# Values as the stationary operand, in two halves of the array's columns, in attentions A and C

## The reference

```python
def gqa_attend(q, k, v, mask=None, sink=None):
    s = jnp.einsum("btkgd,bskd->bkgts", q, k).astype(jnp.float32) * (q.shape[-1] ** -0.5)
    ...
    if sink is not None:
...
    else:
        p = jax.nn.softmax(s, axis=-1)
    o = jnp.einsum("bkgts,bskd->btkgd", p.astype(v.dtype), v)
```

## Time and profile before

| | us |
|---|---|
| median of 3 runs (5578.72 to 5581.25) | 5580.46 |
| the profiled execution | 5575.79 |
| its span | 5574.2 |
| PE busy | 4813.2 (86%) |
| PEld busy | 4151.0 (74%) |
| DVE busy | 3091.8 (55%) |
| ACT busy | 2596.6 (47%) |
| values' sum of A and C, line 837: 3904 PE records | 468.3 busy |
| transposes' copy on ACT, line 882: 288 | 216.5 busy |
| mean granted clock of PE | 0.935 |

### The profile page before, as it was taken

How to read it: one execution, slowest core, us unless ns; L and a number is a source line. 1 busy time by engine, 2 the same in 40 slices (tenths; PEclk the granted TensorE clock), 3 DMA queues, 4 the chain that set the end, 5 groups by cost and what they waited for, 6 DMA issues and landing times. The chain is left out here.

```text
span 5574.2 us, 82058 instructions
## 1 busy us (share of the span) xinstructions
PE 4813.2 (86%) x28941; PEld 4151.0 (74%) x28941; DVE 3091.8 (55%) x4784; ACT 2596.6 (47%) x3436; POOL 1159.4 (21%) x1097
## 2 busy tenths in 40 slices
PE   5788889889799986899992888999989998599994
PEld 0688878779687875787772888998878777487773
DVE  1655145666544443777766551557663433677775
ACT  0444245556423321777762442555652322477773
POOL 0444200340000001333333441004200000333332
PEclk7899999999899997999996999999989998799997
DMA  8533462313433364899986533424153325799997
GB/s 371 193 94 97 165 213 59 80 47 100 155 124 145 143 217 144 332 397 397 397 330 239 171 95 92 109 57 109 50 159 132 134 90 205 259 397 397 397 397 285
DMA packets 597494, 1111.13 MB, mean 199 GB/s; under 512 B 112560, under 2 KB 295632, under 8 KB 589104
## 3 DMA queue, kind: packets, MB, share of 16 engines
q1 hardware_dynamic: 551760, 956.16, 49.4%
q0 software_dynamic: 29504, 94.50, 4.3%
q10 hardware_dynamic: 16032, 57.88, 2.6%
HBM read 907.97 MB, written 200.45 MB: 199 GB/s over the span
## 5 line engine op out<-in xcount | busy, mean ns | idle before, releaser
L658 PE MATMUL project_proj_acc<-project_w_split,project_hT 128*128 128x256 f32 x5472 | 726.8, 293 | 0.0
L658 PEld LDWEIGHTS project_proj_acc<-project_w_split,project_hT 128*128 128x128 f32 x5472 | 696.2, 199 | 0.3 <-issue 0.2
L1538 PE MATMUL merge_acc<-merge_hT,merge_w_split 128*128 128x512 f32 (+1 forms) x2880 | 641.3, 377 | 36.4 <-DMA merge_hT<-hT 30.4
L1538 PEld LDWEIGHTS merge_acc<-merge_hT,merge_w_split 128*128 128x128 f32 x2880 | 506.6, 191 | 146.7 <-issue 29.7
L2185 DVE TENSOR_TENSOR experts_w_gate<-experts_raw_gate,experts_w_gate 128x2048 fp32r<-128x2048 f32 x148 | 373.5, 2531 | 356.1 <-ACT experts_w_gate L2137 355.9
L937 DVE TENSOR_REDUCE attend_stat<-attend_scores 128x1 f32<-128x1280 f32 (+2 forms) x288 | 305.9, 1062 | 325.2 <-PE attend_scores L852 324.2
L2122 POOL TENSOR_TENSOR experts_w_down<-experts_raw_down,experts_w_down 128x2048 fp32r<-128x2048 f32 x74 | 361.4, 4884 | 534.3 <-ACT experts_w_down L2137 534.3
L837 PE MATMUL attend_out_acc<-attend_values,attend_probsT 128*128 128x64 f32 x3904 | 468.3, 271 | 0.1
L837 PEld LDWEIGHTS attend_out_acc<-attend_values,attend_probsT 128*128 128x128 f32 x3904 | 459.3, 192 | 0.4 <-ACT attend_probsT L882 0.4
L2232 PE MATMUL experts_gate_acc<-experts_w_gate,experts_rowsT 128*128 128x512 f32 x1776 | 438.2, 402 | 12.3 <-DVE experts_rowsT L2190 6.0
L2246 PE MATMUL experts_result_acc<-experts_w_down,experts_hiddenT 128*128 128x512 f32 x1776 | 436.8, 401 | 12.2 <-DVE experts_w_down L2185 12.2
(11 more groups left out here) (207 smaller groups left out, 8079.1 us busy)
## 6 DMA issues: line engine op xcount, KB each, us to landing
experts_raw_gate<-in_w_exp_gate_dram SPq DMA_DIRECT2D x148, 1024.0 KB, 13.9
experts_raw_up<-in_w_exp_up_dram SPq DMA_DIRECT2D x148, 1024.0 KB, 12.9
experts_raw_down<-in_w_exp_down_dram SPq DMA_DIRECT2D x148, 1024.0 KB, 11.3
merge_w_raw<-in_w_merge_dram SPq DMA_DIRECT2D x120, 768.0 KB, 6.2
modulation_w_ada<-in_w_ada_dram SPq DMA_DIRECT2D x48, 1024.0 KB, 27.1
qk<-project_staged SPq DMA_DIRECT2D x168, 256.0 KB, 2.3
attend_keys<-qk SPq DMA_DIRECT2D x128, 320.0 KB, 5.7
ye<-experts_result ACTq DMA_DIRECT2D x74, 512.0 KB, 6.2
```

What stands on the lines that cost most here:

```text
L658: m = pe.matmul(acc[s % 4][:, 0:HALF], hT[:, a, k, t * P:(t + 1) * P], w_split[hf][:, c, k, :], start=(i == 0 and k == 0), stop=(i == 2 an ...
L1538: m = pe.matmul(acc[:, b, 0:w], w_split[b][:, a, k, :], hT[:, x, k, 0:w], start=(i == 0 and k == 0), stop=(i == 2 and k == KD - 1))
```

## The change

The values' product changes sides. Before, the transposed probabilities (128 keys x 128 queries) were loaded as the stationary operand and the values (64 columns) streamed through; the sum came out as 128 queries x 64. Now the values (64 columns) are stationary, in the left half of the array's columns for even key tiles and in the right half for odd ones, and the probabilities (128 columns) stream; the sums of the even tiles come out on PSUM partitions 0 to 63 and those of the odd ones on 64 to 127, both transposed. ACT copies this 128x128 block to SBUF (`copy_halves`), and PE multiplies it with two identities on top of each other (`halves`), which adds the two halves and turns the result back to 128 queries x 64 (`turn_back`). The turning back of a step comes in the body of the step three later, and so does `finish` on DVE.

```diff
         def sum_values(i, s):
...
             for j, kt in enumerate(sx.tiles):
-                m = pe.matmul(acc[b][:, 0:HD], probsT[b][:, j, :], values[hb][:, kt, :],
-                              start=(j == 0), stop=(j == sx.n - 1))
+                half = slice(j % 2 * HD, (j % 2 + 1) * HD)
+                m = pe.matmul(acc[b][half, 0:P], values[hb][:, kt, :], probsT[b][:, j, :],
+                              start=(j < 2), stop=(j >= sx.n - 2))
             m.then_inc(pv.sem, 1)
+
+        def turn_back(i, s):
+            g, b = i * NS + s, s % 2
+            pe.wait_ge(hc.sem, hc.done(g))
+            pe.matmul(acc[b][:, P:P + HD], halves_out[b][:, :], halves[:, :], start=True, stop=True
+                      ).then_inc(tb.sem, 1)
...
                 if exists(q):
                     transposes(q, r)
+                q, r = before(i, s - 3)
+                if exists(q):
+                    turn_back(q, r)
                 q, r = before(i, s - 2)
                 if exists(q):
                     sum_values(q, r)
...
+        turn_back(3, NS - 3)
         transposes(3, NS - 1)
         sum_values(3, NS - 2)
         sum_values(3, NS - 1)
+        turn_back(3, NS - 2)
+        turn_back(3, NS - 1)
 
     def scalar(act):
...
+        def copy_halves(i, s):
+            g, b = i * NS + s, s % 2
+            act.wait_ge(pv.sem, pv.done(g))
+            if later(g, 2):
+                act.wait_ge(tb.sem, tb.done(g - 2))
+            act.copy(halves_out[b][:, :], acc[b][:, 0:P]).then_inc(hc.sem, 1)
+
         def body(i):
             for s in range(NS):
                 g, b, sx = i * NS + s, s % 2, steps[s]
                 q, r = before(i, s - 1)
                 if exists(q):
                     copy_out(q, r)
+                q, r = before(i, s - 3)
+                if exists(q):
+                    copy_halves(q, r)
                 act.wait_ge(nb.sem, nb.done(g))
...
-            dve.wait_ge(pv.sem, pv.done(g))
+            dve.wait_ge(tb.sem, tb.done(g))
...
-            dve.tensor_scalar(out[hb][:, s % nq, :], acc[b][:, 0:HD], stat[:, k, 3:4], None, ALU.mult
+            dve.tensor_scalar(out[hb][:, s % nq, :], acc[b][:, P:P + HD], stat[:, k, 3:4], None, ALU.mult
                               ).then_inc(yd.sem, 1)
...
-                q, r = before(i, s - 2)
+                q, r = before(i, s - 3)
                 if exists(q):
                     finish(q, r)
...
+        else:
+            dve.wait_ge(const_in.sem, const_in.done(0))
+            dve.tensor_tensor(halves[:, :], ident[:, 0:HD], ident[:, HD:P], ALU.add).then_inc(halves_ready.sem, 1)
```

More of the change, by code:

```diff
@@ L697 @@
 Attention = namedtuple("Attention", "sync_first sync sync_last tensor scalar vector gpsimd qk pv yd last y_out")
-AttentionBuffers = namedtuple("AttentionBuffers", "const_in ident keys queries values probs probsT out stat scores acc")
+AttentionBuffers = namedtuple("AttentionBuffers", "const_in ident keys queries values probs probsT out stat scores acc "
+                              "halves halves_out")
 def attend_gqa(nc, io, scr, l, nq, st, shared, banded, first=None, before_it=None):
@@ L706, in attend_gqa @@
     tag = "c" if banded else "a"
-    ident, keys, queries, values, probs, probsT, out, stat, scores, acc = (
+    ident, keys, queries, values, probs, probsT, out, stat, scores, acc, halves, halves_out = (
         shared.ident, shared.keys, shared.queries, shared.values, shared.probs, shared.probsT, shared.out,
-        shared.stat, shared.scores, shared.acc)
+        shared.stat, shared.scores, shared.acc, shared.halves, shared.halves_out)
     k_in, q_in, v_in, y_out = ([st.dma(f"{tag}_{n}{b}") for b in range(2)] for n in (
         "keys_loaded", "queries_loaded", "values_loaded", "out_stored"))
-    qk, mx, nb, ex, tr, ca, cv, pv, sm, rc, yd = (st.event(f"{tag}_{n}") for n in (
+    qk, mx, nb, ex, tr, ca, cv, pv, hc, tb, sm, rc, yd = (st.event(f"{tag}_{n}") for n in (
         "scores_done", "row_max", "bias_ready", "exp_done", "probs_transposed", "copied_by_act", "copied_by_dve",
-        "values_summed", "denominator", "reciprocal", "out_ready"))
+        "values_summed", "halves_copied", "turned_back", "denominator", "reciprocal", "out_ready"))
     const_in = shared.const_in
+    halves_ready = None if banded else st.event("two_identities_ready")
     if banded:
@@ L870, in tensor @@
             pe.wait_ge(const_in.sem, const_in.done(0))
+            pe.wait_ge(halves_ready.sem, halves_ready.done(0))
         bodies(pe, body)
+        turn_back(3, NS - 3)
         transposes(3, NS - 1)
@@ L901, in scalar @@
         bodies(act, body)
+        copy_halves(3, NS - 3)
         copy_out(3, NS - 1)
+        copy_halves(3, NS - 2)
+        copy_halves(3, NS - 1)
     def vector(dve):
@@ L958, in vector @@
             dve.wait_ge(const_split.sem, const_split.done(2))
+        else:
+            dve.wait_ge(const_in.sem, const_in.done(0))
+            dve.tensor_tensor(halves[:, :], ident[:, 0:HD], ident[:, HD:P], ALU.add).then_inc(halves_ready.sem, 1)
         bodies(dve, body)
         copy_out(3, NS - 1)
+        finish(3, NS - 3)
         finish(3, NS - 2)
@@ L1248, in stage_attend @@
             [st.sb(f"out{b}", [P, nq, HD]) for b in range(2)], st.sb("stat", [P, 4, 8]),
-            [st.ps(f"scores{b}", [P, 1536]) for b in range(2)], [st.ps(f"out_acc{b}", [P, 512]) for b in range(2)])
+            [st.ps(f"scores{b}", [P, 1536]) for b in range(2)], [st.ps(f"out_acc{b}", [P, 512]) for b in range(2)],
+            st.sb("two_identities", [P, HD]), [st.sb(f"halves_out{b}", [P, P]) for b in range(2)])
         a = attend_gqa(nc, io, scr, l, nq, st, shared, False)
```

## The result

| | before | changed |
|---|---|---|
| median of 4 runs | 5579.63 us (5578.72 to 5581.25) | 5832.06 us (5827.87 to 5843.62) |
| ratio to before, 95% interval | 1 | 1.0455 (1.0437 to 1.0473) |
| profiled execution | 5575.8 us | 5829.71 us |
| its span | 5574.2 us | 5828.1 us |

The change costs 252.4 us by the medians and 253.9 us by the two spans; the forecast was +284 us, to 5864 us. First the page of the changed kernel, its totals: PE, whose sums with the values were to become shorter, is busy for 4818.3 us (4813.2 before), 83% of a span that has grown.

The account below looks back on a forecast made before the run. PE was taken as the bound, busy for 95 to 99% of the attention stretches read. The terms 128 + 121 + 38 + 10 + 3 - 16 = +284 us gave 5864 us on the median's level, range 5755 to 5990.

Parts of the forecast that it names:

- The wait: In each attention step PE stops after the transposes until ACT copies probabilities, then halves: 2.57 us to turning back in A.
- The theory: PE waits for ACT's halves' copy, queued behind a copy needing PE's transposes; the order costs the time, not the copy's work.
- 128 full steps of A: Attention A, steps of 10 key tiles: 5.49 us against 4.49, +1.00 us each, +128 us.
- 96 and 32 steps of C: Attention C: steps of 5 tiles +1.26 us each, +121 us; steps of 4 tiles +1.2 us each, +38 us.
- context steps and ends: 32 context steps of 2 tiles at +0.3 us, +10 us; uncovered ends of four passes through A or C, +3 us.
- the queries' wait: Layer 0, second pair of heads: PE's 16.35 us wait nearly goes because PE arrives later, -16 us.
- the drain: Entering and leaving the halves on PE: a group's tail of 0.19 us, twice in each step.
- The lower end: Entering and leaving the halves cost nothing: the sum 109 us smaller, 5755 us.
- No overlap: Rival in the values' sum: passes in the two halves go one after another; 6057 us, chance 0.08.
- seen loads: Milder rival in the values' sum: each 64-column load is seen, 56 ns; 5979 us, chance 0.06.
- The clock falls: Rival in A: PE's idle time drops its clock to 1.2 GHz, about 4 us a step; 6376 us, chance 0.06.
- The wait is covered: Rival: ACT has the halves in time; full A step 4.01 us, -61 us; C loses 29 us; 5548 us, chance 0.04.

Follow-up runs that it names:

- e1: Experiment 1: the changed kernel with PE's turning back of step s-3 moved behind the values' sum of s-2, ACT's order kept; 5568.2 us, ratio 0.9983.
- e2: Experiment 2: the changed kernel with ACT copying the halves ahead of the probabilities, PE's order kept; 5526.72 us, ratio 0.991.
- e6: Experiment 6: the changed kernel with a second copy of the halves on ACT, to a spare buffer, ahead of the one that counts; 5874.24 us.
- experiment 7: The same extra ACT copy of the halves, added to the e2 kernel; 5527.95 us, ratio 0.9913.
- experiment 4: The changed kernel with two neighbouring tiles' values (128 columns) loaded, array never divided, computing other numbers, for times alone; 5950.69 us.
- experiment 3: The changed kernel with every key tile's pass in the left half, none beside another, turned back with a 64x64 identity; 6010.73 us.
- e9: On top of e5, SP issues the second pair's queries ahead of B's first loads, in layer 0 alone; 5497.7 us, ratio 0.9858.
- e5: Attention A as in e2, attention C as in the kernel before; 5515.06 us, ratio 0.9894, and once more 5512.14 us, ratio 0.9889.
- e8: On top of e5, SP issues what A's second pair of heads needs ahead of B's first loads, in both layers; 5507.0 us, ratio 0.988.

## Why the prediction was right, and where it was 30 us too high

**The wait.** Its place, its releaser and its size were as worked out: ACT's copy 1.29 us after the transposes, the halves' copy 0.91 behind it, 265 to 273 ns long (0.27), 1.27 us idle ("about 1.3"). Only the hand-over from ACT to PE was 0.05 us, not 0.10. The theory rests on experiments 1, 2, 6 and 7. Moving either end of the wait by one place brings back all the loss. More work at that place adds to it, and the same work elsewhere adds nothing.

**The sum against the spans.** The forecast was +284, the two spans differ by 253.9.

| term | forecast | measured |
|---|---|---|
| 128 full steps of A | +1.00 each, +128 | +0.91, +116.5 |
| 96 and 32 steps of C | +121 and +38 | 16 heads by +8.99, +143.8 |
| context steps and ends | +10 and +3 | +5.2, what is left |
| the queries' wait | -16 | -11.6 |

*A.* A step was to take 5.49 us and takes 5.40: 0.05 less at the hand-over, 0.035 less from turning back to values (0.37 for 0.405), 0.025 less from the values to the scores (1.24 for 1.265), and 0.02 more for the scores. The term that was mis-sized is the drain. I took the whole tail of a group, 0.19 us, twice. By experiment 4 the halves cost 0.10 on entering and 0.12 on leaving. Another 0.055 and 0.05 are lost there without halves too (0.27 for 0.215 and 2.20 for 2.15), which I had counted at nothing; so the sum came out 0.06 too high where the drain alone was 0.16 too high. That these two misses nearly cancel is luck. The lower end, no drain at all, was not the case either. The Trainium skill, TensorEngine Tiling (Array Packing), "Key Properties", has a change of the tiling mode drain TensorE; by experiment 4 the change of shape does cost time, about a tenth of a microsecond each way. That the engine empties in it is shown by no run here.

*C.* The inner step rose by 1.15 us, not 1.26 (1.55 to the turning back for 1.61, then 0.37 for 0.405, and 0.79 for 0.835). For a step of 4 tiles I had taken +1.2, and by the step that was the larger miss. Two of these stand together where one head ends and the next begins. PE's transposes around such a place in the kernel before, and then in the changed one:

```profile
4093.65 0.71 PE L826 MATMUL attend_scores<-attend_ident,attend_probs 128*128 128x128 f32 x5
...
4105.15 0.71 PE L826 MATMUL attend_scores<-attend_ident,attend_probs 128*128 128x128 f32 x5
```

```profile
4322.69 0.71 PE L830 MATMUL attend_scores<-attend_ident,attend_probs 128*128 128x128 f32 x5
...
4339.70 0.71 PE L830 MATMUL attend_scores<-attend_ident,attend_probs 128*128 128x128 f32 x5
```

These five steps took 11.50 us and take 17.01, +5.51; the head's three others rose by 1.16 each. That is 8.99 us a head of 8 steps, where 6 x 1.26 + 2 x 1.2 = 9.96 was forecast: 15 us too much over 16 heads. If the three steps of 5 tiles among the five rose by 1.16 too, those of 4 tiles rose by about 1.02 each; then some 0.6 of the 0.97 us a head is the steps of 5 tiles, and 0.4 those of 4.

*Context steps and ends.* Together they came to 5.2 us for 13. What was missed: the first three steps of each of the four passes have no step s-3 to turn back, so nothing waits in them, while the sum counted all 288. In A of layer 1 the first two steps by the transposes' starts took 5.79 and 4.92 us before (3479.01, 3484.80, 3489.72) and 5.80 and 4.34 after (3606.08, 3611.88, 3616.22): 0.57 us less together, where two full steps would be 1.8 more. How the remainder divides between context steps and ends was not measured.

*The queries' wait.* Counted from the first scores of A, PE asks for the second pair's queries 13.1 us later than before (760.36 - 4.80 - 657.50 against 761.63 - 16.35 - 660.3), not 16, and they land 1.5 us later: 11.6 us of the wait went instead of 16. That PE is less late than forecast is the same two things, 0.91 for 1.00 and the first steps: up to the third transposes it is 0.4 us later (17.01 us from the first scores, against 16.59), and the rest, 12.7, is 14 steps of 0.91.

**The rivals.** *No overlap* and *seen loads* are out by the 1.24 us of the values' group and by experiment 3: with one half, where passes can't overlap, it is 2.33. *The clock falls* is out: 1.00 from 3620 to 3945, with PE idle or transposing for 2.5 of every 5.4 us. By the Trainium skill, TensorE: Matmul & The Clock Gate, "PE-mode transpose", transposes don't count as busy in the same way; the trace gives no sign of it at this share of them. *The wait is covered* did not happen in the change but in experiments 1 and 2. Its -61 us for the full steps of A stand against 45 us in e1, or 51 if the 6 us by which the queries' wait grows there are put back, and against 63 in e2. For C it was too kind by e1 and too harsh by e2: 2.63 us a step worked out, 2.65 and 2.48 measured, and a loss of 36 and 9 us, not 29. So its 4.01 us, met to the digit in e1, is luck in part: it was worked out for the change's own order on PE, and that is e2's, with 3.87.

## What to carry to other kernels

When a result is handed from PE to another engine and back, look at both queues: an instruction that nobody hurries, one place behind one that waits for PE, makes PE wait for itself, and here that cost 305 us of 5830 with not one instruction more. Matmuls that write half of the array's columns paid in the long group (2.15 to 1.24 us for 20 passes) and didn't in the short ones (1.04 to 0.79 for 10 passes and 0.84 to 0.59 for 8, with 0.24 to 0.37 for turning back). And once a stage is faster, look at the transfers that it now outruns: the order of SP's queue was worth 14 us more (e9 against e5 once more, 5497.7 and 5512.14 us side by side).

## What was not expected of the hardware

- A turning back costs 0.10 us less when PE comes to it without a stall. From turning back to values there are 0.37 us behind a stall of 1.27 us (the change), and 0.27 with no stall ahead (e2). The price of entering the halves is the same in both: what differs is the distance between the two passes of the turning back itself. The second pass of it, in the change, in e2 and in e4:

```profile
682.62 0.28 PE L849 MATMUL attend_out_acc<-attend_two_identities,attend_halves_out 128*128 128x64 f32 x1
...
685.01 0.28 PE L849 MATMUL attend_out_acc<-attend_two_identities,attend_halves_out 128*128 128x64 f32 x1
...
692.00 0.28 PE L849 MATMUL attend_out_acc<-attend_two_identities,attend_halves_out 128*128 128x64 f32 x1
```

  It starts 0.16 us behind the first pass after a stall, with halves or without (682.46 and 691.84), and 0.06 behind it with none (684.95). From there to the values there are 0.21 us with halves in the change and in e2 (682.83 and 685.22), and 0.11 without (692.11). So entering costs 0.10 us each time, and a stall another 0.10. That is why in e2 a step of A takes 3.87 us and an inner one of C 2.48, less than the 4.01 and 2.63 worked out.
- An idle time of 4.80 us ahead of the second pair of heads still drops the clock: the granted clock is 0.50 from 760.36 to 769.50, and the scores take 2.50 us where a full-speed group takes 1.42. The 1.27 us in every step don't, from 3620 to 3945, nor do single waits of 1.27 and 1.25 us for the same queries (e6, e8), behind which the scores take 1.42.
